# Decay rates brought to columns inside a projection tile, the key matrix ahead of the last convolutions, its copy in another region

## Chip, cores and metric

The kernel runs on one core of one Trainium2 chip. The time is the device time of one execution, in microseconds. Each number of a profile comes from one profiled execution of the same program.

## What is computed

One layer of a hybrid decoder for 528 prompt positions and 32 sample tokens, T = 560 columns in all, laid side by side in every tile. After an RMS norm, one projection of 1024 by 2816 gives queries, keys and values of a gated DeltaNet, its gates, and the inputs of a latent attention. What concerns this change is the DeltaNet's preparation:

```python
qkv, z, b, a, c_q, c_kv, k_pe = split_cols(hn @ w_in, IN_SIZES)
qkv_c = silu(causal_conv(qkv, conv_w))          # width 4, per channel
q, k = l2norm(q) * DK ** -0.5, l2norm(k)        # 8 heads of 64
beta, g = sigmoid(b), -exp(a_log) * softplus(a + dt_bias)
g = cumsum(g, axis=-1)                          # within a chunk of 16 (4 for samples)
decay = where(lower, exp(g_i - g_j), 0)
lmat = where(strict, einsum(k_beta, k) * decay, 0)
u, w = triangular_solve(lmat + eye, [v_beta, k_beta * exp(g)])
qk = where(lower, einsum(q, k) * decay, 0)
# then a scan over the chunks with the state of 64 x 64 per head
```

Then come the output projection, attention over a paged cache, an MLP of 1024 by 4096, and the final norm. The kernel's chunk is 16 columns, 35 chunks (NU) in all.

## The kernel before, in words

TensorE computes every projection in tiles of 128 output features. A tile (`weight_tile`, lines 585 to 601) walks over eight contraction steps k. In each, three products (high weight by high input, high by low, low by high; lines 597, 598 and 599) run over two halves of 288 and 272 columns: six products for a step, 48 for a tile. The results stand in two PSUM banks: tile i takes banks 0 and 1 or 2 and 3 by its parity. The order of the tiles is written out by hand in `TILES`; the loop index i below is the place in that list. Places 10, 11, 12 and 13 are the four value tiles (features 8 to 11), places 14, 16 and 17 feed the query norm, 15 the latent, 18 the output gate. The first 19 places (`EARLY`) run in this loop, the remaining gate tiles in pieces (`gate_products`) between the steps of the recurrence.

Weights come by DMA from the SP queue into two RAW buffers. ScalarE rounds them to WH (`weights_high`, line 1232), VectorE takes the difference WL (`weights_low`, line 1740), one matrix for two tiles. TensorE waits for `w_split` at every even place, and for `p_copied` (the bank of two tiles ago was copied out).

For a DeltaNet tile ScalarE copies the banks to XP (five instructions, lines 1431 to 1437), VectorE convolves XP into CV (`convolve`, lines 1923 to 1927, `conv_done`), and ScalarE writes silu(CV) to KQT or, for the values, to VBD (line 1282). Behind some tiles stands small work that prepares the recurrence:

- place 9 to 11: `key_products(0..2)`; ScalarE copies them into KK and KQ (`copy_products`, lines 1304 and 1305, `kk_copied`).
- place 11: `spread_rows(0)`, two products (four passes in the trace) that spread an eight-row table BROW over 128 rows into banks 6 and 7 (line 569).
- place 12: `gates_to_columns`: 16 products with eight contraction rows whose moving operand takes every 16th column of BROW (`BROW[:, :, t:T:CH]`, 175 columns, line 579) into bank 5, then 8 products of 35 or 8 columns (lines 581 and 583), then `spread_rows(1)`. VectorE must have finished the gates' sums (`gates_sums`, last line 1812), ScalarE the second KK and KQ copy.
- place 13: `spread_rows(2)`.
- place 14: `chunk_transposes`, 16 transposes of KK (line 650) that wait for `b_ready`; ScalarE copies them to BU and XU (lines 1339 and 1340), and VectorE solves the triangular systems there (`substitute`, lines 1906 and 1908; `inverted` at its end).

Between these stand, on ScalarE, `rates` (RL from bank 5, two exponentials, lines 1322 to 1326), the decay exponential over TMP (line 1475) and `last_rates` (EGL, EGLS); on VectorE `by_column` (multiplies KK or KQ by banks 6 and 7, line 1862, `col_used`), `masked`, `scaled`, `rate_products`, `decay_differences` (line 1880), `rate_exponents`, `key_matrix` (lines 1890 and 1891, `b_ready`), and `query_matrix` (line 1897, `at_done`). All engines run their queues in program order.

Memory: AT lies at the start of the region r4, where XP0 also lies; BU lies behind AT at `prep_at`, over XP and CV of the convolutions; E16, the stationary tables of line 579, lies at r2, where the output gate ZG is written later.

Of the kernel before, what the change touches and what calls it, by code (L numbers as in the profile page):

```python
# [127 lines left out]
def build(nc, big_at, row_at, a):  # L128
# [93 lines left out]
    EGLS, at = put("EGLS", [P, PAIRS, BS], F32, rows_end - 768)  # L222
    EGL, at = put("EGL", [P, PAIRS, NU], F32, at)
    assert at <= rows_end
    BU, inv_at = put("BU", [NU, CH, P], F32, prep_at)
    XU, at = put("XU", [NU, CH, H, CH], F32, inv_at)
    MU, at = put("MU", [NU, 512], F32, at)
    OR, _ = put("OR", [P, NU + 1, DK], F32, inv_at)
# [111 lines left out]
    with ctx:  # L340
# [31 lines left out]


        SQ0 = {"ckv": 0, "cq": 2, "mlp": 5}
        GROUPS = [(4 * i, min(4 * i + 4, NU)) for i in range(9)]
        ROOT = {"ckv": 1, "cq": 2, "mlp": 3}
        HALF0 = {"out": 10, "mlp": 18}
# [129 lines left out]
        def _(pe):  # L507
# [61 lines left out]
                    last = pe.matmul(PS[:, b, 0:n], row("hexp"), BROW[:, (3, 1, 4)[x], c:c + n], start=True, stop=True)  # L569
                last.then_inc(sem("col_spread"), 1)  # L570

            def gates_to_columns():

                pe.wait_ge(sem("e16_in"), 16)
                pe.wait_ge(sem("dve_step"), DVE_STEP["gates"])
                pe.wait_ge(sem("qk_inverted"), 2)
                pe.wait_ge(sem("kk_copied"), 2)
                for t in range(CH):
                    pe.matmul(PS[:, 5, 0:5 * NU], row("e16", t), BROW[:, :, t:T:CH], start=(t == 0), stop=(t == CH - 1))  # L579
                for p in range(PAIRS):  # L580
                    pe.matmul(PS[:, 5, 192 + NU * p:192 + NU * p + NU], row("bpair", p), BROW[:, 1, CH - 1:T:CH],
                              start=True, stop=True)
                    last = pe.matmul(PS[:, 5, 352 + BS * p:352 + BS * p + BS], row("bpair", p),
                                     BROW[:, 1, NP + TS - 1:T:TS], start=True, stop=True)
                last.then_inc(sem("pe_step"), 1)

            def weight_tile(w, mt, moving, banks, halves, ready=None):

# [149 lines left out]
            for i, m in enumerate(TILES[:EARLY]):  # L738
                if i % 2 == 0 and i or i == 1:
                    pe.wait_ge(sem("w_split"), i // 2 + 1)  # L740
                if i >= 2:
                    pe.wait_ge(sem("p_copied"), i - 1)
                b = 2 * (i % 2)
                if i == 0:
                    first_tile()
                else:
                    last = weight_tile(i // 2, i % 2, (XH, XL), (b, b + 1), HALVES)
                    last.then_inc(sem("tile_done"), 1)
                if i < 5:
                    if i == 0:  # L750
                        pe.wait_ge(sem("act_step"), ACT_STEP["cstate_copied"])
                    else:
                        pe.wait_ge(sem("ht_copied"), 2 * i)
                    token_transposes(i, XN[:, i, :], (6, 7), "ht_done")
                if i == 2:
                    pe.wait_ge(sem("cst_in"), 32)
                if 2 <= i < 10:
                    head_sums(i - 2)
                if 9 <= i < 12:
                    key_products(i - 9)  # L760
                if i == 11:
                    spread_rows(0)
                elif i == 12:
                    gates_to_columns()
                    spread_rows(1)
                elif i == 13:
                    spread_rows(2)
                elif i == 14:
                    for x in range(4):
                        chunk_transposes(x)  # L770
                elif i == 16:
                    pe.wait_ge(sem("xu_copied"), 4)
                    sum_squares("ckv", 2)
                elif i == 17:
                    pe.wait_ge(sem("root"), ROOT["ckv"])
                    for u in range(3):
                        keys_values(u)
                elif i == 18:
                    pe.wait_ge(sem("kv_copied"), 3)
                    sum_squares("cq", 3)  # L780
                    solved_transposes(0)
                    solved_transposes(1)
# [431 lines left out]
        def _(act):  # L1214
# [206 lines left out]
            for i, m in enumerate(TILES[:EARLY]):  # L1421
# [4 lines left out]
                if m < 12:  # L1426
                    d = CONV.index(m)
                    if d >= 2:
                        act.wait_ge(sem("conv_done"), d - 1)
                    x = XP[d % 2]  # L1430
                    act.activation(x[:, 3:291], PS[:, b, 0:288], ACT.Copy)
                    act.activation(x[:, 291:3 + NP], PS[:, b + 1, 0:240], ACT.Copy)
                    samples = x[:, 3 + NP:].rearrange("p (b k) -> p b k", b=BS)
                    act.activation(samples[:, :, 3:7],
                                   PS[:, b + 1, 240:272].rearrange("p (b k) -> p b k", b=BS), ACT.Copy)
                    act.activation(samples[:, :, 0:3], CST3[:, m, :].rearrange("p (b k) -> p b k", b=BS), ACT.Copy)
                    act.activation(TAIL[:, m, :], PS[:, b + 1, 224:272], ACT.Copy).then_inc(sem("p_copied"), 1)
                    if i < 5:
                        for x in (2 * i, 2 * i + 1):
                            act.wait_ge(sem("ht_done"), x + 1)  # L1440
                            act.activation(four_tiles(x, HT), transposed(6 + x % 2, i), ACT.Copy)\
                                .then_inc(sem("ht_copied"), 1)
                else:
                    if m < 15:
                        dst, f = CQ[:, m - 12, :], ACT.Copy
                    elif m < 17:
                        dst, f = LATT[:, m - 15, :], ACT.Copy
                        if m == 15:
                            act.wait_ge(sem("at_done"), 1)
                    elif m == 17:  # L1450
                        dst, f = SPEC[:, :], ACT.Copy
                    else:
                        dst, f = ZG[:, m - 18, :], ACT.Silu
                    for (c, n), x in zip(HALVES, (b, b + 1)):
                        last = act.activation(dst[:, c:c + n], PS[:, x, 0:n], f)
                    last.then_inc(sem("p_copied"), 1)
                if i and TILES[i - 1] < 12:
                    silu_out(CONV.index(TILES[i - 1]))
                if 1 <= i < 9:
                    head_squares(i - 1)  # L1460
# [8 lines left out]
                    copy_products(1)  # L1469
                elif i == 12:  # L1470
                    copy_products(2)
                    rates()
                elif i == 13:
                    act.wait_ge(sem("dve_step"), DVE_STEP["decay_diff"])
                    act.activation(TMP[:, :, :], TMP[:, :, :], ACT.Exp, scale=-1.0).then_inc(sem("act_step"), 1)
                    last_rates()
                elif i == 14:
                    act.wait_ge(sem("silu_done"), 12)
                    for x in range(4):
                        copy_chunks(x)  # L1480
                elif i == 15:
                    act.wait_ge(sem("p_copied"), 16)
                    squares("ckv", lambda d: LATT[:, d, :], 2)
                elif i == 16:
                    root("ckv", 2, KV)
                    act.wait_ge(sem("col_used"), 3)
                    lay_keys(0)
                    lay_keys(1)
                elif i == 17:
                    for u in range(3):  # L1490
                        copy_kv(u)
                    act.wait_ge(sem("p_copied"), 18)
                    squares("cq", lambda d: CQ[:, d, :], 3)
                elif i == 18:
                    act.wait_ge(sem("lat_done"), 2)
                    root("cq", 3, QL)
                    gate_out(0)
                    copy_wt(0)
                    copy_wt(1)
                    gate_out(1)  # L1500
# [232 lines left out]
        def _(dve):  # L1733
# [159 lines left out]

            def query_matrix():

                by_column(KQ, 2)
                dve.tensor_tensor(AT[:, :, :], KQ[:, :, :], decays[1], ALU.mult).then_inc(sem("at_done"), 1)

            def substitute(lo, hi):
# [30 lines left out]
                last.then_inc(sem("conv_done"), 1)  # L1930

            for i, m in enumerate(TILES[:EARLY]):
                if i % 2 == 0 and i < 16:
                    weights_low(i // 2 + 1)
                if m < 12:
                    convolve(CONV.index(m), m)
                if i == 7:
                    invert_norms(0)
# [5 lines left out]
                elif i == 12:  # L1944
                    dve.wait_ge(sem("kk_copied"), 3)
                    by_column(KK, 0)
                    rate_products()
                    link(masked(KK, "m_lower"))
                    decay_differences()
                    masked(KQ, "m_updiag")  # L1950
                    link(scaled(KK, 10))
                    link(scaled(KQ, 3))
                    rate_exponents()
                elif i == 13:
                    key_matrix()
                    query_matrix()

            dve.wait_ge(sem("xu_copied"), 4)
            substitute(1, 8)
# [494 lines left out]
```

## Time and profile before

| | us |
|---|---|
| median of 3 runs | 1036.35 (1035.49 to 1036.37) |
| profiled execution, own time | 1033.08 |
| span in the profile | 1031.3 |
| TensorE products busy | 981.3 (95%) |
| VectorE busy | 514.1 (50%) |
| ScalarE busy | 446.4 (43%) |
| GpSimd busy | 157.1 (15%) |
| mean granted TensorE clock | 0.981 |

The page cuts the span in 40 slices of 25.8 us. The granted clock reads 9 (nine tenths or more of 2.4 GHz) in most of them, 6 in the sixth (129 to 155 us) and 8 in a few: these spent a part at 1.2 GHz. The busy time of TensorE counts products of any size as busy, and at either clock: it tells where the engine had something, not how fast it went.

### The profile page before, as it was taken

What the parts mean: (1) busy time and instruction counts of PE and PEld (TensorE: products, weight loads), DVE (VectorE), ACT (ScalarE), POOL (GpSimd) and SP (SyncE); (2) the same over time, 40 slices, a digit from 0 to 9 for tenths busy, and PEclk for the clock granted to TensorE, in tenths of its full rate; (3) what the DMA queues carried; (4) which work ended last, traced back from release to release, by engine and by line L of the source; (5) the groups of instructions that cost most, each with busy time, mean ns of one, the idle gap of its engine ahead of it and who ended that gap; (6) DMA issues with size and microseconds to landing.
All of it is one profiled execution on the core that took longest, in us unless ns stands there. A gap on an engine that the chain in (4) does not pass through costs nothing.

```text
span 1031.3 us, 20653 instructions
## 1 busy us (share of the span) xinstructions
PE 981.3 (95%) x8604; PEld 850.7 (82%) x8604; DVE 514.1 (50%) x977; ACT 446.4 (43%) x964; POOL 157.1 (15%) x257
## 2 busy tenths in 40 slices
PE   4999999999989999899999899999999999999997
PEld 3988899877757556566665799999999999999996
DVE  5655867565575485355454532633343234334423
ACT  5545637566646675344444423431232134113312
POOL 1020500255511201345541000000000000000000
PEclk9999969999999999899999899999999999999998
DMA  7312111220024501477672321422222222223202
GB/s 247 116 51 83 43 42 42 58 52 11 2 65 116 208 1 33 178 252 261 242 241 91 118 83 41 144 82 83 85 100 102 82 83 83 82 85 100 104 1 87
DMA packets 31655, 102.58 MB, mean 99 GB/s; under 512 B 14023, under 2 KB 14967, under 8 KB 25218
## 3 DMA queue, kind: packets, MB, share of 16 engines
q1 hardware_dynamic: 22346, 63.50, 18.9%
q0 software_dynamic: 9216, 37.75, 10.6%
q8 instruction: 69, 1.13, 0.4%
q14 instruction: 24, 0.20, 0.1%
HBM read 96.45 MB, written 4.22 MB: 98 GB/s over the span
## 4 chain that ended last, share of the span: by engine, by line
PE 87%; DVE 6%; ACT 3%; issue 2%; DMA 1%; SPq 0%; DVEq 0%; ACTq 0%
PE PS L597 17%; PE PS L599 17%; PE PS L598 17%; PE PS L1086 7%; PE PS L1097 3%; PE PS L1123 3%; PE PS L732 2%; PE PS L1106 1%; PE PS L805 1%; PE PS L836 1%; PE PS L888 1%; DMA RAW<-in_w_stream 1%; PE PS L987 1%; PE PS L579 1%; PE PS L706 1%
## 5 line engine op out<-in xcount | busy, mean ns | idle before, releaser
L597 PE MATMUL PS<-XH,WH 128*128 128x272 f32 (+1 forms) x928 | 271.2, 292 | 1.8 <-DVE WL L1740 1.8
L599 PE MATMUL PS<-XH,WL 128*128 128x272 f32 (+1 forms) x928 | 270.4, 291 | 0.0
L598 PE MATMUL PS<-XL,WH 128*128 128x272 f32 (+1 forms) x928 | 269.5, 290 | 0.0
L597 PEld LDWEIGHTS PS<-XH,WH 128*128 128x128 f32 x928 | 175.9, 190 | 6.8 <-issue 4.2
L598 PEld LDWEIGHTS PS<-XL,WH 128*128 128x128 f32 x928 | 176.1, 190 | 0.0
L1232 ACT ACTIVATE WH<-RAW 128x2048 fp32r<-128x2048 f32 x46 | 88.0, 1913 | 203.1 <-PE PS L599 203.0
L599 PEld LDWEIGHTS PS<-XH,WL 128*128 128x128 f32 x928 | 175.8, 189 | 0.0
L597 PE MATMUL PS<-NH,WH 128*128 128x272 f32 x512 | 149.1, 291 | 0.8 <-DVE WL L1740 0.8
L599 PE MATMUL PS<-NH,WL 128*128 128x272 f32 x512 | 147.6, 288 | 0.0
L598 PE MATMUL PS<-NL,WH 128*128 128x272 f32 x512 | 146.6, 286 | 0.0
L1740 DVE TENSOR_TENSOR WL<-RAW,WH 128x2048 fp32r<-128x2048 f32 (+1 forms) x48 | 108.1, 2252 | 65.3 <-ACT WH L1232 64.2
L2234 DVE TENSOR_TENSOR HT<-HT,PS 128x272 f32<-128x272 f32 x80 | 31.4, 433 | 137.8 <-PE PS L599 137.8
L597 PEld LDWEIGHTS PS<-NH,WH 128*128 128x128 f32 x512 | 96.3, 188 | 1.3 <-DVE WL L1740 1.0
L598 PEld LDWEIGHTS PS<-NL,WH 128*128 128x128 f32 x512 | 96.1, 188 | 0.3
L599 PEld LDWEIGHTS PS<-NH,WL 128*128 128x128 f32 x512 | 96.2, 188 | 0.0
L2354 POOL DMA_INDIRECT CN<-in_cache,IDX x64 | 60.5, 946 | 129.2 <-PE PS L1123 55.8
L1086 PEld LDWEIGHTS PS<-CST,CN 128*128 128x128 f32 x512 | 59.8, 146 | 23.9 <-DVE CT L2187 14.7
L2187 DVE COPY CT<-PS 128x512 f32<-128x512 f32 x64 | 44.2, 691 | 63.2 <-PE PS L1086 63.2
L1086 PE MATMUL PS<-CST,CN 128*128 128x128 f32 x512 | 70.8, 284 | 2.2 <-DVE CT L2187 1.9
L1648 ACT ACTIVATE CT<-PS 128x512 f32<-128x512 f32 x64 | 38.2, 596 | 56.6 <-PE PS L1086 56.3
L2262 DVE SCALAR_TENSOR_TENSOR AR<-PS,RSTD 128x272 f32<-128x272 f32 x64 | 25.2, 435 | 59.8 <-PE PS L599 59.8
L1705 ACT ACTIVATE AR<-AR 128x544 f32<-128x544 f32 x32 | 20.8, 649 | 61.1 <-DVE AR L2262 61.1
(331 smaller groups left out, 1498.3 us busy)
## 6 DMA issues: line engine op xcount, KB each, us to landing
RAW<-in_w_stream SPq DMA_DIRECT2D x47, 1024.0 KB, 4.8
XN<-in_hin SPq DMA_DIRECT2D x4, 512.0 KB, 6.5
out_y_p<-YO SPq DMA_DIRECT2D x4, 512.0 KB, 2.7
CST<-in_big SPq DMA_DIRECT2D x1, 1132.5 KB, 13.4
SS<-in_sstate SPq DMA_DIRECT2D x1, 1024.0 KB, 5.3
out_ssm_s<-SS SPq DMA_DIRECT2D x4, 256.0 KB
CN<-in_cache,IDX POOLq DMA_INDIRECT x64
WQN<-in_wq SPq DMA_DIRECT2D x3, 256.0 KB, 5.9
```

The lines of the kernel that those rows point to most:

```text
L597: pe.matmul(PS[:, b, 0:n], wh, xh[:, k, c:c + n], start=(k == 0), stop=False)
L598: pe.matmul(PS[:, b, 0:n], wh, xl[:, k, c:c + n], start=False, stop=False)
L599: last = pe.matmul(PS[:, b, 0:n], wl, xh[:, k, c:c + n], start=False, stop=(k == DT - 1))
L1086: last = pe.transpose(PS[:, CT_BANKS[x % 4], P * j:P * j + P], src, ident)
L1097: last = pe.matmul(PS[32 * b:32 * b + 32, bank, :], QF[:, g, c, 32 * b:32 * b + 32], CT[4 * c + b][:, :], start=(c == 0), stop=False)
L1123: last = pe.matmul(PS[32 * b:32 * b + 32, 6, 0:KV], PTE[n % 2][:, j, 32 * b:32 * b + 32], CN[n % 4][b][:, j, 0:KV], start=(j == 0), stop=( ...
L1232: act.activation(WH[w % 2][:, :, :], RAW[w % 2][:, :, :], ACT.Copy).then_inc(sem("w_high"), 1)
L1648: act.activation(CT[u][:, :], PS[:, CT_BANKS[(9 * n + u) % 4], :], ACT.Copy).then_inc(sem("ct_act"), 1)
L1740: return dve.tensor_tensor(out, full, high.bitcast(F32), ALU.subtract)
L2187: dve.tensor_copy(CT[u][:, :], PS[:, CT_BANKS[(9 * n + u) % 4], :]).then_inc(sem("ct_dve"), 1)
L2234: last = dve.tensor_tensor(HT[:, j, c:c + n], HT[:, j, c:c + n], PS[:, b, 0:n], ALU.add)
L2354: pool.indirect_dma_start(CN[n % 4][b][:, :, :].rearrange("p r d -> p (r d)"), None, KEYS, bass.IndirectOffsetOnAxis(IDX[:, 4 * n + b:4 * ...
```

## The change

- `gates_to_columns` is split. Its 16 strided products (`gate_columns(k)`) are issued inside the tile at place 13, ahead of the contraction steps k = 2 to 7, three, three, three, three, two and two of them. The waits that stood ahead of it stand ahead of k = 2. The 8 small ones (`gates_of_pairs`) and `spread_rows(1)` follow behind the tile at place 13 instead of 12.
- `spread_rows(2)` is issued inside the tile at place 14, ahead of k = 3, instead of behind place 13.
- VectorE leaves the convolutions of places 12 and 13 until after the key matrix; `weights_low(8)` stands between them. The decay differences come before the mask of KQ, `key_matrix` before the scaling of KQ, `query_matrix` after the first of the two convolutions.
- ScalarE does `rates` at place 13 instead of 12, and the last two silu passes behind the four copies of the transposes at place 14. At place 18 the root of the query norm comes ahead of the gate's silu copy, which now also waits for `inverted`.
- BU moves to r2 (over E16, and where ZG is written later); XU and what follows keep their places.

```diff
@@ memory @@
-    BU, inv_at = put("BU", [NU, CH, P], F32, prep_at)
+    BU, at = put("BU", [NU, CH, P], F32, r2)
+    assert at <= r3
+    inv_at = prep_at + CH * P * 4
@@ TensorE @@
+        GATE_SPLIT = [(0, 0), (0, 0), (0, 3), (3, 6), (6, 9), (9, 12), (12, 14), (14, 16)]
-            def gates_to_columns():
-                pe.wait_ge(sem("e16_in"), 16)
-                pe.wait_ge(sem("dve_step"), DVE_STEP["gates"])
-                pe.wait_ge(sem("qk_inverted"), 2)
-                pe.wait_ge(sem("kk_copied"), 2)
-                for t in range(CH):
+            def gate_columns(k):
+                if k == 2:
+                    pe.wait_ge(sem("e16_in"), 16)
+                    pe.wait_ge(sem("dve_step"), DVE_STEP["gates"])
+                    pe.wait_ge(sem("qk_inverted"), 2)
+                    pe.wait_ge(sem("kk_copied"), 2)
+                for t in range(*GATE_SPLIT[k]):
                     pe.matmul(PS[:, 5, 0:5 * NU], row("e16", t), BROW[:, :, t:T:CH], start=(t == 0), stop=(t == CH - 1))
+            def gates_of_pairs():
                 for p in range(PAIRS):
...
+            def last_spread(k):
+                if k == 3:
+                    spread_rows(2)
...
-                    last = weight_tile(i // 2, i % 2, (XH, XL), (b, b + 1), HALVES)
+                    between = gate_columns if i == 13 else last_spread if i == 14 else None
+                    last = weight_tile(i // 2, i % 2, (XH, XL), (b, b + 1), HALVES, between)
...
-                elif i == 12:
-                    gates_to_columns()
+                elif i == 13:
+                    gates_of_pairs()
                     spread_rows(1)
-                elif i == 13:
-                    spread_rows(2)
@@ ScalarE @@
                     else:
+                        act.wait_ge(sem("lat_done"), 2)
+                        root("cq", 3, QL)
+                        act.wait_ge(sem("inverted"), 1)
                         dst, f = ZG[:, m - 18, :], ACT.Silu
...
-                if i and TILES[i - 1] < 12:
+                if 1 <= i < 13 and TILES[i - 1] < 12:
                     silu_out(CONV.index(TILES[i - 1]))
...
                     copy_products(2)
+                elif i == 13:
                     rates()
-                elif i == 13:
                     act.wait_ge(sem("dve_step"), DVE_STEP["decay_diff"])
...
                 elif i == 14:
-                    act.wait_ge(sem("silu_done"), 12)
                     for x in range(4):
                         copy_chunks(x)
+                    silu_out(10)
+                    silu_out(11)
...
-                    act.wait_ge(sem("lat_done"), 2)
-                    root("cq", 3, QL)
                     gate_out(0)
@@ VectorE @@
             def query_matrix():
-                by_column(KQ, 2)
+                dve.wait_ge(sem("conv_done"), 11)
...
-                if i % 2 == 0 and i < 16:
+                if i % 2 == 0 and i < 14:
                     weights_low(i // 2 + 1)
-                if m < 12:
+                if m < 12 and i < 12:
                     convolve(CONV.index(m), m)
...
                     by_column(KK, 0)
+                    link(masked(KK, "m_lower"))
                     rate_products()
-                    link(masked(KK, "m_lower"))
                     decay_differences()
-                    masked(KQ, "m_updiag")
+                    link(masked(KQ, "m_updiag"))
                     link(scaled(KK, 10))
+                    key_matrix()
                     link(scaled(KQ, 3))
+                    by_column(KQ, 2)
                     rate_exponents()
-                elif i == 13:
-                    key_matrix()
+                    convolve(10, TILES[12])
                     query_matrix()
+                    weights_low(8)
+                    convolve(11, TILES[13])
```

## Rows read from the trace of the kernel before

**Rows 1.** The page, part 1: busy us, share of the span, instructions.

```profile
PE 981.3 (95%) x8604; PEld 850.7 (82%) x8604; DVE 514.1 (50%) x977; ACT 446.4 (43%) x964; POOL 157.1 (15%) x257
```

**Rows 2.** Waits of PE, whole span: total us, times, longest.

```profile
PE PS L579 <- ACT KQ L1305: 2.0, 1, 2.0
...
PE PS L650 <- DVE KQ L1862: 1.0, 1, 1.0
...
PE PS L706 <- ACT WT L1386: 0.6, 1, 0.6
```

**Rows 3.** Windows, PE: stretch, length, busy (count), granted clock, DMA, GB/s.

```profile
124.40:126.30 1.90, 0.00 (x0) 1.00 0.00 0
126.40:128.10 1.70, 1.70 (x6) 1.00 0.00 0
128.10:141.30 13.20, 13.20 (x48) 0.50 0.25 79
141.30:145.10 3.80, 3.80 (x17) 0.50 0.02 6
...
150.50:156.80 6.30, 6.30 (x49) 1.00 0.00 1
```

**Rows 4.** Line 579: count, ns min/median/max, first and last start.

```profile
L579 PE MATMUL PS<-BROW,E x32: 467/468/509, 126.4 to 135.6; 8*128 8x175 f32 x32
```

**Rows 5.** Timeline of PE, 135 to 160 us: start, us, what, count.

```profile
135.90 0.45 PE L581 MATMUL PS<-BROW,ROWS 8*128 8x35 f32 x2
...
139.14 2.21 PE L569 MATMUL PS<-BROW,ROWS 8*128 8x288 f32 x4
141.28 0.61 PE L597 MATMUL PS<-XH,WH 128*128 128x288 f32 x1
...
149.17 0.28 PE L599 MATMUL PS<-XH,WL 128*128 128x272 f32 x1
149.38 1.21 PE L569 MATMUL PS<-BROW,ROWS 8*128 8x288 f32 x4
150.52 0.40 PE L597 MATMUL PS<-XH,WH 128*128 128x288 f32 x1
150.76 0.29 PE L598 MATMUL PS<-XL,WH 128*128 128x288 f32 x1
...
157.99 1.93 PE L650 MATMUL PS<-CST,KK 128*35 128x128 f32 x16 [1.03 <-DVE KQ L1862]
159.68 0.38 PE L597 MATMUL PS<-XH,WH 128*128 128x288 f32 x1
```

**Rows 6.** Windows of PE again, later in the span.

```profile
404.50:408.00 3.50, 3.24 (x81) 1.00 0.02 5
408.00:411.40 3.40, 3.36 (x16) 0.50 0.45 133
...
414.80:418.20 3.40, 1.25 (x10) 1.00 1.01 401
418.30:425.00 6.70, 6.03 (x24) 0.50 0.73 302
```

**Rows 7.** Timeline of DVE and ACT around the key matrix.

```profile
125.91 0.33 ACT L1305 ACTIVATE KQ<-PS 128x192 f32<-128x192 f32 x1
...
153.14 1.28 ACT L1475 ACT_TABLE_LOAD   x1
...
155.61 0.74 DVE L1890 TENSOR_TENSOR KK<-KK,TMP 128x560 f32<-128x560 f32 x1 [1.52 <-ACT TMP L1475]
...
166.68 0.35 DVE L1906 TENSOR_TENSOR MU<-BU,XU 35x112 f32<-35x112 f32 x1 [5.86 <-ACT XU L1340]
```

**Rows 8.** Timeline of DVE, PE and ACT between the solve and the recurrence.

```profile
188.40 0.27 DVE L1908 TENSOR_TENSOR XU<-XU,MU 35x112 f32<-35x112 f32 x1
...
190.90 1.18 PE L658 MATMUL PS<-CST,XU 35*128 35x35 f32 x16
...
195.73 1.28 ACT L1418 ACT_TABLE_LOAD   x1
```

## The prediction

> **What bounds the kernel now.** I read the busy times first. TensorE is busy 981.3 of 1031.3 us, twice any other engine [rows 1], so only what moves TensorE's own queue can move the end. The waits of that queue come next: around the changed code they are 2.0 us ahead of the strided gate products (line 579), 1.0 us ahead of the transposes of the key matrix, and 0.6 us for a copy ahead of the recurrence [rows 2]. Waits alone are worth 3.6 us.
>
> The windows show the larger thing. Tile 12 ends at 124.4, the queue then waits, and after 1.7 us of strided products the granted clock falls from 2.4 to 1.2 GHz. It stays there for 17.0 us, from 128.1 to 145.1: 13.2 us of eight-row products without a pause, then the first 3.8 us of tile 13, where a dense product takes 3.8 / 17 = 0.224 us. At the full clock a tile's 48 take 6.3 us, or 0.131 each [rows 3]. So the question is what the new order does to the clock, as much as what it does to the waits.
>
> **The change, part by part.** I follow TensorE from the end of tile 12 (124.4) to the start of tile 15 (159.7 [rows 5]), 35.3 us now. First the sum with the clock at 2.4 GHz throughout:
>
> - The wait. Tile 13 now begins at once. Its first two steps (12 products, 1.6 us) end at 126.0; the strided ones still need ScalarE's second KQ copy, which ends at 126.24 [rows 7], and begin at 126.4 as now. 0.4 us is left of 1.9.
> - The 32 strided passes (16 products of two passes). Their starts run from 126.4 to 135.6, 0.30 apart. The pace is the same where the clock still read 1.00 (six passes in 1.7 us) and at 0.50 [rows 3, 4]. I take 9.5 us at either clock.
> - Six insertions into a tile, a new cost. Four contiguous eight-row passes take 1.14 us at the full clock (149.38 to 150.52) and 2.14 at half (139.14 to 141.28) [rows 5]. If a pass doubles and the rest doesn't, a pass is 0.25 and 0.14 is fixed. The product ahead of the insertion is spaced 0.21 and the one behind it 0.24 instead of 0.13, together 0.19. So 0.33 for each, 2.0 for six. The bounds are nothing and 3.
> - Tile 13's own 48 products: 6.3 us.
> - The 16 small passes (lines 581, 583): 3.24 us at 1.2 GHz, 135.90 to 139.14 [rows 5]. They are short, so I take half, 1.6; between 1.6 and 3.2.
> - The second spread, 1.3 us with its edges; tile 14, 6.3 us; the third spread inside it, 1.3 us.
> - The transposes, 1.7 us (157.99 to 159.68 [rows 5]). Their wait of 1.0 goes, see below.
>
> The sum is 0.4 + 9.5 + 2.0 + 6.3 + 1.6 + 1.3 + 6.3 + 1.3 + 1.7 = 30.4 us instead of 35.3: 4.9 less.
>
> What is late next there? The spread ends 145.5, the differences and clamps take about 1.7, the exponential 1.1, two passes of 0.74 end in b_ready [rows 7], near 150 (the others are estimated from this 0.74 by their size); scaling and spreading over KQ end near 151.8. TensorE is done with tile 14 near 153.1. The margin is 1.3 us. The Exp table load of 1.28 us, which now stands between a silu and the exponential [rows 7], goes, since no silu runs between the rates and the decay.
>
> VectorE's two convolutions, `weights_low(8)` and the last silu passes move behind the key matrix. Queued behind them on VectorE is the substitution. It waited 5.86 us for ScalarE's copies of the transposes [rows 7], which covers most of two convolutions; what is left shifts with TensorE. BU in its other region frees these convolutions from the copies and costs no instruction. The new wait of ScalarE on `inverted` holds the gate copy. Now the solve ends at 188.7, 2.2 us before TensorE takes it up at 190.9 [rows 8], and the copy comes later still: the wait costs nothing, unless the solve slips by over 2 us against TensorE. One table load of 1.28 goes because root comes ahead of silu [rows 8]. It frees the 0.6 us wait [rows 2]; TensorE's pieces of the gate tile may wait 0.3 for the copied bank instead. I take 0.6 less. DMA is untouched: no load is reordered.
>
> At the full clock all this gives 5.5 us less, 1030.9.
>
> **The clock.** It fell at 128.1, 3.7 us after the last dense product. It did not return during 13.2 us of eight-row products back to back, and it did 3.8 us into dense ones [rows 3]. Yet 3.4 us of sixteen 128-row passes at 1.2 GHz, from 408.0, came ahead of a return: by 414.8 it read 1.00. So eight-row products don't do for the clock what 128-row products do, however full the queue. And it fell twice where the engine had work: at 408.0 behind 3.5 us of short 16-column products that read as 93% busy, and at 418.2 behind 3.4 us with ten products and 1.25 us of work [rows 6]. In the new tile 13 a step takes six strided passes, six dense products and an insertion, 1.8 + 0.8 + 0.3 = 2.9 us, of which 0.8 is dense, for 16 us on end, and 2.9 us of eight-row work follow with nothing dense at all. By kind of work that is nearer to the stretches ahead of the three falls than to any that kept the clock. The likeliest case is that it falls inside tile 13.
>
> When? The fall came 3.7 us after dense work ended and the return 3.8 us after it began, so I take 4 us after 126.0, near 130, with one step done. From there a dense product costs 0.093 more (0.224 against 0.131): 30 of them 2.8 us. The 16 small passes cost 1.6 more, the spread 1.0 more. Tile 14 is at 1.2 GHz for 4 us (17 products, 1.6 us lost) if the clock returns before the inserted spread, and to its end (48 products 4.5, the spread 1.0, the transposes estimated 1.0: 6.5 us) if the eight-row passes at k = 3 put that off. I take the middle, 4.0. Together 9.4 lost.
>
> Forecast: -4.9 + 9.4 - 0.6 = +3.9 us. Against the profiled execution's own 1033.08 (span 1031.3 and 1.8 around it) this is 1037.0. That execution was 3.3 us faster than the median; I add the change to the median: 1036.35 + 3.9 = **1040.3**. Its own range, from 1.6 to 6.5 for tile 14 and 1 us each way for the insertions, is 1036.9 to 1043.8.
>
> **The Trainium skill** ("TensorE: Matmul & The Clock Gate", "Why this matters for your kernels") asks to avoid idle gaps between bursts of matmuls, and tells of a clock that follows business. By it a queue kept full would keep 2.4 GHz, the first rival below. The rows speak against it for eight-row products. It states in "SBUF — State Buffer", under "Door 1: The DMA port swizzle", that reads which change the 16-byte line each time pay a penalty; line 579 reads every 16th fp32. The spacing of 0.30 at granted 1.00 agrees.
>
> **The rivals.**
> - The clock holds throughout: 1030.9. For it: little is left of the 2 us wait, and dense products come every 2.6 us. Against it: the 13.2 us in which eight-row work did not restore the clock. 12 in 100.
> - The clock holds in tile 13 and falls behind it, in the 2.9 us of small passes and spread. The spread and tile 14 lose 0 to 1.0 and 1.6 to 4.5: about 3.5. -5.5 + 3.5 = -2.0, 1034.4. 20 in 100.
> - The strided passes go at 0.15 when the clock is up. They would save 32 x 0.15 = 4.8 more: 1026. Against it: the six passes at 1.00 [rows 3]. 4 in 100.
> - The clock holds but a new wait decides: the chain from the rates to the key matrix slips by more than its 1.3 us of margin, each us beyond it one us of TensorE; with two table loads, 2.6 - 1.3 = 1.3 us, 1032.2, and about 1034 with a brief fall. 7 in 100.
> - The forecast, slower than before: 57 in 100. It decides from the point where the clock falls before half of tile 13 is done; then the loss exceeds the 5.5 us won.
>
> **The numbers.** About 0.2%, 2.1 us, is what a measurement can tell from no change: 1034.3 to 1038.4. The forecast's case gives 53 slower and 4 same; the second 9 faster, 11 same; the full clock and the fast passes 16 faster; the late chain 5 faster and 2 same. So faster 0.30, same 0.17, slower 0.53. The range is 1031.0 to 1044.0: it covers the forecast's own and reaches to the rival at the full clock; what is left out are the fast passes and part of that rival.
>
> **What would show it.** In the new profile the gap ahead of line 579 should be near 0.4 us and the one ahead of line 650 gone: right whatever the clock does. The windows should read 0.50 from about 130 until tile 14 or 15, with dense spacing 0.23 inside tile 13. Tile 15 would begin near 164.2 with the fall, near 154.8 without. Strided passes 0.30 apart at granted 1.00 prove that term, 0.15 refute it. The forecast is wrong if the clock reads 1.00 through tile 13.

## The result, and the profile after

The changed kernel is slower: 1043.93 us median (1041.1 to 1045.4) against 1035.8 for the kernel before on the same chip, a ratio of 1.0075 with the 95% interval 1.0059 to 1.0092, or 7.8 us (6.1 to 9.5). The profiled execution took 1043.78 with a span of 1042.0.

The page's part 1, then the granted clock of its part 2 (40 slices, tenths of 2.4 GHz):

```profile
PE 994.8 (95%) x8604; PEld 858.7 (82%) x8604; DVE 513.7 (49%) x977; ACT 441.6 (42%) x960; POOL 157.4 (15%) x257
...
PEclk9999958999999999899999899999999999999999
```

The share of TensorE's busy time is the same as in [rows 1], 95%: that number says nothing here. Its waits, as in [rows 2]:

```profile
PE PS L583 <- ACT KQ L1316: 0.4, 1, 0.4
```

Line 583 is line 579 of before. The 2.0 us ahead of the strided products are 0.4 now, and no wait of 0.2 us or more stands ahead of the transposes or for line 706's copy. So the change does what it says: 3.2 us of waits are gone. ScalarE has four instructions fewer than in [rows 1], 960, and they are table loads. The windows of PE (stretch, length, busy with count, granted clock, DMA, GB/s), to be read against [rows 3], show what came in their place:

```profile
124.40:126.30 1.90, 1.52 (x12) 1.00 0.00 0
126.40:128.00 1.60, 1.60 (x6) 1.00 0.00 0
128.00:147.50 19.50, 19.50 (x64) 0.50 0.16 55
147.50:153.10 5.60, 5.60 (x21) 0.50 0.00 0
153.10:165.50 12.40, 12.40 (x47) 0.50 0.00 0
165.60:166.30 0.70, 0.70 (x7) 1.00 0.05 12
```

The clock is at 1.2 GHz for 37.5 us, from 128.0 to 165.5, where it was 17.0 us. That is most of tile 13, the small products, the second spread and nearly all of tile 14. The timeline of PE in it (start, us, what, count), for one step of tile 13 and the end of the stretch, to be read beside [rows 5]:

```profile
126.37 1.99 PE L583 MATMUL PS<-BROW,E 8*128 8x175 f32 x6 [0.45 <-ACT KQ L1316]
...
129.99 2.12 PE L583 MATMUL PS<-BROW,E 8*128 8x175 f32 x6
132.04 0.61 PE L609 MATMUL PS<-XH,WH 128*128 128x288 f32 x1
...
133.73 2.12 PE L583 MATMUL PS<-BROW,E 8*128 8x175 f32 x6
...
147.55 0.64 PE L588 MATMUL PS<-BROW,ROWS 8*128 8x35 f32 x2
...
150.99 2.21 PE L572 MATMUL PS<-BROW,ROWS 8*128 8x288 f32 x4
153.13 0.61 PE L609 MATMUL PS<-XH,WH 128*128 128x288 f32 x1
...
166.36 1.91 PE L662 MATMUL PS<-CST,KK 128*35 128x128 f32 x16
168.02 0.38 PE L609 MATMUL PS<-XH,WH 128*128 128x288 f32 x1
```

A step of tile 13 lasts 129.99 to 133.73, 3.74 us. Tile 15 begins at 168.0 instead of 159.7, 8.3 us late.

### The profile page after: what moved, and what is told of

Same layout as the page of the kernel before. It is cut to its first block, busy times and chain, and to the rows that moved or that the text cites. A ratio compares the mean times of both kernels' runs of the same rounds, so it can differ in the third digit from the quotient of the medians.

```text
span 1042.0 us, 20650 instructions
## 1 busy us (share of the span) xinstructions
PE 994.8 (95%) x8604; PEld 858.7 (82%) x8604; DVE 513.7 (49%) x977; ACT 441.6 (42%) x960; POOL 157.4 (15%) x257
## 4 chain that ended last, share of the span: by engine, by line
PE 89%; DVE 6%; ACT 2%; issue 2%; DMA 1%; SPq 0%; DVEq 0%; ACTq 0%
PE PS L609 18%; PE PS L611 17%; PE PS L610 17%; PE PS L1097 7%; PE PS L1108 3%; PE PS L1134 3%; PE PS L744 3%; PE PS L1117 1%; PE PS L816 1%; PE PS L847 1%; PE PS L899 1%; PE PS L583 1%; DMA RAW<-in_w_stream 1%; PE PS L537 1%; PE PS L998 1%
## 5 line engine op out<-in xcount | busy, mean ns | idle before, releaser
L609 PE MATMUL PS<-XH,WH 128*128 128x272 f32 (+1 forms) x928 | 275.2, 297 | 1.7 <-DVE WL L1753 1.7
L611 PE MATMUL PS<-XH,WL 128*128 128x272 f32 (+1 forms) x928 | 273.3, 295 | 0.0
L610 PE MATMUL PS<-XL,WH 128*128 128x272 f32 (+1 forms) x928 | 272.3, 293 | 0.0
L609 PEld LDWEIGHTS PS<-XH,WH 128*128 128x128 f32 x928 | 178.5, 192 | 9.4 <-issue 6.9
L610 PEld LDWEIGHTS PS<-XL,WH 128*128 128x128 f32 x928 | 178.9, 193 | 0.0
L611 PEld LDWEIGHTS PS<-XH,WL 128*128 128x128 f32 x928 | 178.7, 193 | 0.0
```

The costliest lines, as they stand in the source:

```text
L609: pe.matmul(PS[:, b, 0:n], wh, xh[:, k, c:c + n], start=(k == 0), stop=False)
L610: pe.matmul(PS[:, b, 0:n], wh, xl[:, k, c:c + n], start=False, stop=False)
L611: last = pe.matmul(PS[:, b, 0:n], wl, xh[:, k, c:c + n], start=False, stop=(k == DT - 1))
```

## The experiments

Two theories stood against each other. A: the clock falls because eight-row products do little for it, however full the queue is; the change lets the dense products run in that company. B: it falls from the many switches and short gaps, whatever the rows. A third possibility is that the loss is on the other engines, whose order was changed as well. The kernel before took from 1032.2 to 1035.8 us (medians) in the four sets of runs, each on its own chip, so each ratio is to runs of the kernel before on the same chip, and the us beside it are that ratio times its median there.

**Is it the splitting, or the rest?** `before_split` has TensorE's new order in the kernel before, all else untouched:

```diff
...
+                    between = gate_columns if i == 13 else last_spread if i == 14 else None
...
-                elif i == 12:
-                    gates_to_columns()
+                elif i == 13:
+                    gates_of_pairs()
                     spread_rows(1)
-                elif i == 13:
-                    spread_rows(2)
```

> The kernel before with TensorE's new order alone: strided products inside tile 13, the third spread inside tile 14; the other engines and BU as before. If the splitting is the loss, the clock falls near 128 and returns in or behind tile 14, as in the changed kernel, and the time is 1044 to 1048, since the key matrix then waits for the late rates as well. The rival, that it takes the reordering of the others for the loss, gives less than 1038.

Measured: 1.0094 (1.0079 to 1.0108), 9.7 us slower than before. Its windows of PE:

```profile
126.50:128.00 1.50, 1.50 (x6) 0.98 0.00 0
128.00:165.00 37.00, 37.00 (x128) 0.50 0.08 29
```

The clock is low for 37.5 us here too, and the transposes begin at 166.35 without a wait (166.36 in the changed kernel): the late rates, which I had expected to cost something more, did not hold TensorE up. The splitting alone makes the whole loss. The counterpart keeps everything of the change but TensorE's order. The first attempt, `after_lump`, left ScalarE's rates behind tile 13:

```diff
-                    between = gate_columns if i == 13 else last_spread if i == 14 else None
+                    between = None
+                elif i == 12:
+                    for k in range(2, DT):
+                        gate_columns(k)
+                    gates_of_pairs()
+                    spread_rows(1)
                 elif i == 13:
-                    gates_of_pairs()
-                    spread_rows(1)
+                    spread_rows(2)
```

> The changed kernel with TensorE's order of the kernel before: the 16 strided products in one block behind tile 12, the small ones and the second spread behind them, the third spread behind tile 13. ScalarE's, VectorE's order and the place of BU are those of the change. This prices everything but the splitting. If the splitting and its clock are the whole loss, the time is that of the kernel before less 1.0 for the wait ahead of the transposes and 0.6 ahead of the recurrence: 1034 to 1035. Rival: the reordering on the other engines costs too; then it is above 1036.

Measured: 1.0043 (1.0029 to 1.0058), a miss. Its waits show why:

```profile
PE PS L572 <- DVE TMP L1897: 2.9, 1, 2.9
```

The third spread waited for the decay differences, these for the rates, and these stood on ScalarE behind the copy of tile 13. Behind that wait the clock was at 1.2 GHz a second time, from 150.8 to 157.6. With ScalarE's `rates()` back at place 12 (`after_lump2`):

```diff
                     copy_products(2)
+                    rates()
                 elif i == 13:
-                    rates()
```

> As the run with TensorE's old order in the changed kernel, but ScalarE's rates are at place 12 again, where they need no later tile. In the first such run TensorE waited 2.9 us ahead of the third spread, since the rates stood behind tile 13 on ScalarE, and the clock fell a second time; both were of that mixture and neither of the change. Now that wait and the second fall should be gone, the wait ahead of the transposes too: 1.0 to 1.6 us less than the kernel before. If it is slower than before, the order on ScalarE and VectorE has a price of its own.

Measured: 0.9984 (0.9975 to 0.9994), 1.6 us less than before, inside what was expected. The transposes begin at 156.75 without a wait, and the clock is low for as long as before, 17.1 us:

```profile
128.00:145.10 17.10, 17.10 (x64) 0.50 0.18 63
```

So the rest of the change (convolutions behind the key matrix, BU elsewhere, root ahead of silu) is worth a gain of about 1.6 us (0.6 to 2.6), and the splitting costs 9 to 10: 7.8 + 1.6 = 9.4 with it, 9.7 without.

**Is it the rows?** `after_pad128` gives E16, ROWS and BROW 128 partitions. GpSimd sets all to zero early, the same instructions as before fill rows 0 to 7, and the products read 128 rows. Every result, column and count is unchanged.

```diff
-    E16, at = put("E16", [H, CH * P], F32, r2)
+    E16, at = put("E16", [P, CH * P], F32, r2)
...
-    BROW, rows_end = put("BROW", [H, 5, T], F32, at)
+    BROW, rows_end = put("BROW", [P, 5, T], F32, at)
...
+            pool.memset(ROWS[:, :], 0.0).then_inc(sem("vbd_zero"), 1)
+            pool.memset(BROW[:, :, :], 0.0).then_inc(sem("vbd_zero"), 1)
...
+            pool.wait_ge(sem("ht_done"), 10)
+            pool.memset(E16[:, :], 0.0).then_inc(sem("vbd_zero"), 1)
```

> The changed kernel with every eight-row product (strided gates, small gate products, spreads) widened to 128 contraction rows: rows 8 to 127 of both operands are set to zero by GpSimd early on, so the results are the same and the count, columns and order of products too. Theory A (the clock falls because eight-row work does little for it, however full the queue): the granted clock stays 1.00 from 120 to 170 us, tile 15 starts near 155 instead of 168, and the time is 12 to 13 us below the changed kernel, 4 to 6 below the kernel before (about 1031). With it the pace of the strided passes at full clock shows: 0.30 us if the stride sets it, 0.15 if the clock does; in the latter case another 4 us less. Theory B (the clock falls from the many switches and short gaps between kinds of work, whatever their rows): the fall stays at about 128, and the time is that of the changed kernel, near 1044.

Measured: 0.9935 (0.992 to 0.995), 6.7 us faster than before and, by the two ratios, 14.5 us below the changed kernel; a little more than the 4 to 6 and 12 to 13 expected. Windows of PE:

```profile
124.00:126.00 2.00, 1.36 (x11) 1.00 0.00 0
126.00:140.00 14.00, 13.98 (x67) 1.00 0.22 77
140.00:143.10 3.10, 3.10 (x25) 1.00 0.00 0
143.10:150.00 6.90, 6.90 (x52) 1.00 0.00 0
```

The clock stays at 2.4 GHz through the same products in the same order, with the same wait ahead of them (0.7 us here). B falls. The added rows hold nothing but zeros on both sides, so it is the rows in use that count here, not the data in them. The passes are still 0.295 apart: six in a step of 128.63 to 131.18, with the dense products taking the other 0.78. In the kernel before (`before_pad128`, the same edit):

> The same widening in the kernel before, whose order is untouched. Theory A: the 17 us at 1.2 GHz shrink to one short fall or none (the 2 us wait stays), the small gate products take 1.6 instead of 3.2, the spread 1.1 instead of 2.1, tile 13 loses nothing: 4 to 5 us less than before (about 1031.5). So A says that rows bring most of what the change was to bring, without it. Theory B: the fall at 128 follows the 2 us wait and stays, but it may end earlier; 0 to 3 us less.

Measured: 0.9977 (0.9965 to 0.9989), 2.4 us less than before. A had said 4 to 5, B 0 to 3: the time by itself speaks for B, and only the trace decides. Windows of PE:

```profile
123.60:125.80 2.20, 0.06 (x1) 1.00 0.00 0
125.80:127.50 1.70, 1.68 (x6) 0.86 0.00 0
127.50:130.90 3.40, 3.40 (x14) 0.57 0.00 0
131.00:137.00 6.00, 6.00 (x32) 1.00 0.52 175
137.70:141.00 3.30, 3.30 (x14) 0.55 0.03 7
```

A fall comes behind the wait, at 127.0, as B had it too, but the clock is back by 131 in the middle of the block of widened strided products, where the eight-row block had not brought it back in 13 us. It falls again at 137.7, behind 1.7 us of small products of 35 and 8 columns and 0.7 us into the second spread. Short columns stood ahead of the fall at 408.0 in [rows 6] as well. But no run varies them alone, and in the widened changed kernel the same small products, behind dense ones, bring no fall: what brings this second one stays open. The two falls, and a wait of 1.4 us ahead of the transposes, are what the estimate lacked.

With 32 rows (`after_pad32`; `[32, ...]` in place of `[P, ...]`):

> The widening to 32 rows instead of 128. If what the array does for the clock goes with the rows used, 32 rows do little: the fall near 128 stays, and the time is within 2 us of the changed kernel (some 9 above before). If any full 32-row part of the array counts as the whole, the clock holds as with 128 rows, 6 us below before.

Measured: 1.006 (1.0038 to 1.0081), 6.2 us slower than before.

```profile
126.00:130.00 4.00, 4.00 (x17) 1.00 0.00 0
130.20:160.00 29.80, 29.80 (x101) 0.50 0.10 36
```

The fall comes 2 to 3 us later than with eight rows and ends 4 to 5 us sooner. Whether that is the rows or the execution, one trace of each can't tell, and the times (6.2 and 7.8 us slower) overlap. What is shown is that 32 rows do not count as 128. This run also clears the rest of the edit: it has the same memsets and the same waits for them as `after_pad128`, and the clock falls all the same.

**Which of the eight-row products matter?** `after_pad_strided` widens the strided ones only; the spreads are shown, the small products are cut to eight rows in the same way:

```diff
-                    last = pe.matmul(PS[:, b, 0:n], row("hexp"), BROW[:, (3, 1, 4)[x], c:c + n], start=True, stop=True)
+                    last = pe.matmul(PS[:, b, 0:n], row("hexp")[0:H, :], BROW[0:H, (3, 1, 4)[x], c:c + n], start=True, stop=True)
...
```

> Only the strided products are widened to 128 rows; the 8 small products and the three spreads keep eight. It splits the loss: the clock should hold through tile 13, and the 2.9 us of eight-row work behind it then shows what it does alone. If that is enough for a fall, the clock drops near 142 and returns within tile 14 or 15, and the time is 1 to 5 us above the fully widened kernel; if not, within 0.5 us of it. In both cases most of the 17 us between the changed kernel and the fully widened one should be gone.

Measured: 0.995 (0.9934 to 0.9966), 5.2 us faster than before, against 6.7 with all widened. Windows of PE:

```profile
126.50:140.00 13.50, 13.50 (x70) 1.00 0.23 79
140.00:142.00 2.00, 2.00 (x16) 1.00 0.00 0
142.00:145.80 3.80, 3.80 (x19) 0.62 0.00 0
```

This is the prediction's second rival, made to order: the clock holds in tile 13 and falls behind it, at 142.9, for 3.4 us. The price is 1.5 us by the two ratios, with intervals that overlap, so its size is an estimate. The bulk of the loss was with the strided products.

**Would a thinner mixture do?** `after_thin` keeps eight rows, but issues the 16 strided products over tiles 13 and 14:

```diff
-        GATE_SPLIT = [(0, 0), (0, 0), (0, 3), (3, 6), (6, 9), (9, 12), (12, 14), (14, 16)]
+        THIN = [[(0, 0), (0, 0), (0, 1), (1, 2), (2, 3), (3, 4), (4, 5), (5, 6)],
+                [(6, 7), (7, 8), (8, 9), (9, 10), (10, 12), (12, 13), (13, 15), (15, 16)]]
...
```

> The changed kernel, eight rows, but the 16 strided products are spread over tiles 13 and 14 (one per contraction step, two in two of them); the small ones, the second spread follow tile 14, the third spread is inside tile 15, the transposes follow tile 15, and ScalarE's rates and copies move one place. So 0.8 of some 1.8 us of a step is dense instead of 0.8 of 2.9. If the mixture decides, the clock holds through tile 13 and 14 and falls, if at all, behind tile 14 for the 2.9 us of eight-row work there: 1031 to 1035 beside 1033, well below the changed kernel. Rival: any eight-row insertion is enough; then it is at 1.2 GHz from about 128 on for two tiles and the time is at or above the changed kernel's.

Measured: 1.0091 (1.0072 to 1.0109), 9.4 us slower than before, against -2 to +2 expected: a miss. The windows:

```profile
126.00:144.60 18.60, 18.60 (x85) 1.00 0.17 58
144.80:172.00 27.20, 27.20 (x97) 0.50 0.00 0
```

With one strided product to a step the clock holds for 18.6 us, so an insertion as such does not bring the fall. It falls at 144.8, right behind the four passes of the first step with two (143.17 to 144.6). Then follow the rest of tile 14, the small products, two spreads and nearly all of tile 15 at 1.2 GHz, 27.3 us. That fits the theory that the mixture decides, and I misjudged where this one stood; with a single fall to go by, it is a fit and no proof. The time has another part that the edit brought in. Up to tile 16 the trace is 8.7 us late (174.7 instead of 166.0); then TensorE waits for ScalarE's squares, which now stand behind the copies and silu passes, and the clock falls once more, for 3.4 us:

```profile
184.43 2.77 PE L538 MATMUL PS<-TMP,CST 128*128 128x288 f32 x8 [3.33 <-ACT TMP L1232]
```

At the recurrence it is 13.2 us late, in an execution (1046.14 us) that was the slowest of four.

**What sets the pace of the strided passes?** `after_contig128` is the widened changed kernel with neighbouring columns; the rates brought to columns are then other values.

```diff
-                    pe.matmul(PS[:, 5, 0:5 * NU], row("e16", t), BROW[:, :, t:T:CH], start=(t == 0), stop=(t == CH - 1))
+                    pe.matmul(PS[:, 5, 0:5 * NU], row("e16", t), BROW[:, 3, t:t + 5 * NU], start=(t == 0), stop=(t == CH - 1))
```

> The changed kernel widened to 128 rows, whose strided products now read 175 neighbouring columns of one row set instead of every 16th; the values brought to columns are then not the rates, all else is as it was. The clock held at 1.00 with the widened strided passes, which still came 0.29 to 0.30 us apart. If the stride sets that pace, the passes come 0.15 to 0.17 apart and the time falls by 4 to 5 us against the widened kernel (about 1022 beside 1033 of before). If it is the weight load or the issue of these passes, they stay at 0.30 and the time stays.

Measured: 0.9876 (0.9859 to 0.9893), 12.8 us less than before and 6.1 below the widened kernel by the ratios, more than the 4 to 5 expected. The instructions of the line, strided (`after_pad128`) and then contiguous (kind, count, ns min/median/max, first and last start):

```profile
L584 PE MATMUL PS<-BROW,E x32: 453/472/515, 126.0 to 139.1; 128*128 128x175 f32 x32
```

```profile
L584 PE MATMUL PS<-BROW,E x32: 309/312/387, 126.4 to 134.9; 128*128 128x175 f32 x32
```

A step takes 1.66 us instead of 2.55 (starts 128.09 and 129.75): with 0.78 for the dense products the six passes have 0.88, 0.147 each, half the strided 0.295. The stride costs 4.6 us in this stretch at the full clock. At 1.2 GHz the strided passes take 0.296, twice 0.147, so I infer that the stride costs nothing there, and that this is why they looked indifferent to the clock; no run has these passes contiguous at 1.2 GHz. The recurrence starts 4.4 us sooner. The remainder lies later in the span: one stretch at 1.2 GHz near 330 lasts 3.4 us instead of 6.8, which is a part of it, and the rest is unexplained.

**A version that beats both.** With 128 rows the dense products around the block should not be needed. `pad128_block` issues all 16 strided products ahead of k = 2, beside a repetition of the widened kernel:

```diff
-        GATE_SPLIT = [(0, 0), (0, 0), (0, 3), (3, 6), (6, 9), (9, 12), (12, 14), (14, 16)]
+        GATE_SPLIT = [(0, 0), (0, 0), (0, 16), (16, 16), (16, 16), (16, 16), (16, 16), (16, 16)]
```

> The widened changed kernel once more, so that the next two are compared with it on one chip: 6 to 7 us below the kernel before.

> The widened changed kernel with all 16 strided products ahead of step k = 2 in one block instead of six portions. In the widened kernel before, the clock came back to 2.4 GHz in the middle of such a block, so with 128 rows the block does not need dense products around it. Then five insertions of about 0.33 us go and it is 1.5 us below the widened kernel with portions, about 1025 beside 1033. Rival: the portions keep the clock up also with 128 rows; then it falls in the block, and the time is 1 to 4 us above the widened kernel.

Measured: 0.9935 (0.9918 to 0.9952) again for the portions, 1027.04 us beside 1033.83; 0.9923 (0.9906 to 0.9939) for the block, 1025.91 us. Windows of the block version:

```profile
124.00:126.00 2.00, 1.41 (x5) 1.00 0.00 0
126.00:136.00 10.00, 10.00 (x43) 1.00 0.30 106
136.00:146.00 10.00, 10.00 (x75) 1.00 0.01 2
```

Here too the clock reads 1.00 throughout. Both beat both kernels, by 7 to 8 us the kernel before. Between them 1.1 us lies inside the intervals, and the trace says that the order is worth nothing: from the first strided pass to the first small one it is 14.2 us in both. First the block, then the portions (`pad128_again`):

```profile
124.59 9.71 PE L584 MATMUL PS<-BROW,E 128*128 128x175 f32 x32 [0.63 <-ACT KQ L1319]
...
138.76 0.31 PE L589 MATMUL PS<-BROW,ROWS 128*128 128x35 f32 x2
```

```profile
126.22 2.00 PE L584 MATMUL PS<-BROW,E 128*128 128x175 f32 x6 [0.66 <-ACT KQ L1319]
...
140.41 0.32 PE L589 MATMUL PS<-BROW,ROWS 128*128 128x35 f32 x2
```

The five insertions, from which I had expected 1.5 us, cost nothing with 128 rows. The block's trace is earlier by 1.6 us, but it is so already where the products begin. What matters is that they begin two steps into tile 13, not behind a 2 us wait (where the widening alone gained 2.4 us), and that they use all rows.

## Why the prediction was right, and where it was short

**Side and mechanism: right, and shown.** The clock falls inside tile 13 and comes back near the end of tile 14; `before_split` and `after_lump2` place the loss in the splitting, `after_pad128` in its rows. The size was not right: the change is twice the 3.9 us forecast, just outside the forecast's own bounds of 0.5 to 7.4, and the time, 1043.93, lies at the very end of the stated range.

**The sum at the full clock.** The wait left is 0.45 us (0.4 said). The strided passes at 0.30 at either clock hold (0.296 in both). The small passes take 1.7 us at 2.4 GHz (140.20 to 141.90 in `after_pad128`; 1.6 said) and 3.4 at 1.2. The transposes' wait is gone. The recurrence's wait is gone too: tile 15 was 8.3 us late, its first state product (line 788) starts at 207.4 instead of 199.9, 7.5 late; 0.6 was said. The two chains that might have come late did not: in the changed kernel the transposes start 0.13 us behind the last dense product, no wait shown, and none is shown in the widened one either, where they start at 150.05 at the full clock.

**The forecast of 3.9 us against 7.8 measured** (7.5 in the trace up to the recurrence). The prediction set tile 15's start at 164.2 with the fall; it is 168.0. Four of the sum's terms were mis-sized:

- Six insertions, 0.33 each. That came from four contiguous passes at the full clock. At 1.2 GHz a step of 3.74 us holds six passes of 0.296 and six dense products of 0.233, 3.17 together: 0.57 for an insertion, 1.4 us more for six.
- The fall came at 128.0, not near 130. All 36 dense products behind it were at 0.233 instead of 0.131: 3.7 us, not 2.8.
- Tile 14: between 1.6 and 6.5 I took the middle, 4.0. Tile and spread took 13.2 us (153.1 to 166.4), 5.6 more than the 7.6 of the full clock. That is 1.6 us more. The clock came back only near the tile's end, as the upper bound had it; that it was the eight-row spread at k = 3 that put it off is argued, no run has tile 14 without it.
- The small passes: 0.2 more.

These are 4.1 us; the trace has 3.8, since the second spread took 2.1 and not 2.3, and the rest is rounding. The first I had priced at 2.4 GHz, the third between its bounds: the bounds were right, the choice was too kind.

**The rivals.** That the clock holds throughout is refuted: 37.5 us at 1.2 GHz without a pause in the queue. The Trainium skill ("TensorE: Matmul & The Clock Gate", "Why this matters for your kernels") asks only that TensorE be kept busy without idle gaps, and for eight-row work that was not enough here. That a clock that holds would have given 5.5 us or more is borne out, since the widened kernel gains 6.7. The brief fall behind tile 13 is real, but only with widened strided products. Fast strided passes are refuted by 0.295 at granted 1.00, and the reason of their pace is the stride: contiguous reads run at 0.147. This agrees with the penalty that the Trainium skill ("SBUF — State Buffer", "Door 1: The DMA port swizzle") states for each access that crosses to a new line of 16 bytes. The late chain did not occur.

**What the two profiles differ by elsewhere.** The two profiled spans differ by 10.7 us, 3 more than at the recurrence. Later in the changed kernel's trace stand two falls that the trace of before has not:

```profile
305.00:309.00 4.00, 4.00 (x23) 0.57 0.42 82
346.00:350.00 4.00, 4.00 (x14) 0.57 0.98 383
```

Nothing of the change touches that work. It is rather the trace of before that is the odd one. Of the thirteen traces only it and that of `after_thin` have neither fall (`after_lump2`, with TensorE's order of before, has them from 295 and from 336), and its execution was 2.7 us faster than its median. That such stretches differ between executions of one program is shown once: `after_pad128` and `pad128_again` are the same kernel, and near 570 the clock is low for 6.8 us in one and 10.2 in the other. So the two profiles alone would have overstated the loss; the ratio of the timed runs is the number to use.

## What to carry to other kernels

Before moving small products in among dense ones, look at the granted clock around them, not at the busy share: if a stretch of them stands at 1.2 GHz without a pause, they may take the dense work down with them, and each dense product then costs 0.23 instead of 0.13. How much of them a step bears is not settled here: one product did no such harm in ten steps, three did at once. Where such products use few contraction rows, zero rows to fill the 128 can be cheaper than any reordering: here they cost a few GpSimd memsets and turned 7.8 us of loss into 6.7 of gain. When a term has two bounds that depend on the clock, price the whole stretch at the lower clock once a fall is forecast.

## What the runs showed of the hardware that I had not expected

- Rows of zeros hold the clock. The same products with 8, 32 and 128 rows left TensorE at 1.2 GHz for 37.5, 30.7 and 0 us around this place (one trace for the first two, two traces and the block version for the last).
- Widened products bring the clock back on their own: by 131 us in `before_pad128`, in the middle of a block of strided passes. In the same trace it fell again behind 1.7 us of short ones (35 and 8 columns, 128 rows too); behind dense products the same short ones brought no fall.
- An insertion among dense products costs about 0.6 us with eight rows at 1.2 GHz, 0.36 at 2.4 (a step of 1.73 us in `after_thin`, with two passes of 0.296 and 0.78 of dense work), and nothing with 128 rows (six portions and one block both take 14.2 us).
- Reading every 16th fp32 doubles a pass of 175 columns at 2.4 GHz, from 0.147 to 0.295 us. At 1.2 GHz the strided pass takes 0.296, and I infer that the stride is free there.
